# One core, two transformer blocks: the context's norm in the MLP, keys ahead of queries, borders by halves

## What is computed

```python
x = x + jnp.square(jax.nn.relu(h @ mlp_w1[i].astype(dt))) @ mlp_w2[i].astype(dt)
...
mod = (silu_c @ ada_w[i] + ada_b[i])[:, None, :]
mod_c = (silu_cc @ ada_w[i] + ada_b[i])[:, None, :]
...
h = modulate(rmsnorm_2(x, norm1_g[i]), sh1, sc1)
hc = modulate(rmsnorm_2(ctx, norm1_g[i]), csh1, csc1)
...
q, k, v = project(h)
q, k = apply_rope_2d(q, cos, sin), apply_rope_2d(k, cos, sin)
qc, kc, vc = project(hc)
k_all = jnp.concatenate([kc, k], axis=1)
v_all = jnp.concatenate([vc, v], axis=1)
...
x = x + g1 * y
x = x + g2 * swiglu(modulate(rmsnorm_2(x, norm2_g[i]), sh2, sc2), ffn_w_in[i], ffn_w_out[i])
```

## Time and profile before

| what | value |
|---|---|
| median of 3 runs | 2803.95 us (2801.78 to 2805.73) |
| the profiled execution | 2803.94 us, span of its instructions 2802.6 us |
| PE busy | 2633.5 us, 94% of the span |
| DVE, ACT, POOL busy | 1392.8, 910.1, 160.9 us |
| chain that ended last | PE 80%, DVE 11%, ACT 6% |
| mean granted TensorE clock | 0.970 of 2.4 GHz |
| DMA | 265.73 MB moved, mean 95 GB/s |
| TensorE waited for `h_lo` | 12.4 us in 11 waits (L151), 8.5 in 4 (L159) |
| TensorE waited for `w_lo` | 18.6 us in 13 waits |

### The profile page before, as it was taken

How to read it: one execution, slowest core, us unless ns; L and a number is a source line. 1 busy time by engine, 2 the same in 40 slices (tenths; PEclk the granted TensorE clock), 3 DMA queues, 4 the chain that set the end, 5 groups by cost and what they waited for, 6 DMA issues and landing times.

```text
span 2802.6 us, 34040 instructions
## 1 busy us (share of the span) xinstructions
PE 2633.5 (94%) x14886; PEld 2208.8 (79%) x14886; DVE 1392.8 (50%) x1665; ACT 910.1 (32%) x1247; POOL 160.9 (6%) x177
## 2 busy tenths in 40 slices
PE   6998999979999999999979999799999999999998
PEld 4877888878878777887868977678888788788886
DVE  5665544254465346655465257456643454443433
ACT  4332223253334432222332257432222232322222
POOL 0002210000000010000022000010000100100001
PEclk9999999999999999999989999989999999999999
DMA  3220002212333234453222100055532222223231
GB/s 117 76 90 17 28 6 76 91 61 66 115 106 121 76 119 164 154 205 125 103 84 73 63 16 1 28 181 202 207 120 90 90 91 91 90 90 105 91 101 65
DMA packets 39301, 265.73 MB, mean 95 GB/s; under 512 B 4256, under 2 KB 4640, under 8 KB 8944
## 3 DMA queue, kind: packets, MB, share of 16 engines
q1 hardware_dynamic: 29520, 205.67, 21.3%
q0 software_dynamic: 8256, 55.41, 5.7%
q10 hardware_dynamic: 1376, 2.47, 0.2%
HBM read 261.43 MB, written 2.10 MB: 94 GB/s over the span
## 4 chain that ended last, share of the span: by engine, by line
PE 80%; DVE 11%; ACT 6%; issue 2%; POOL 0%; DMA 0%; DVEq 0%; ACTq 0%
PE bank L142 79%; ACT w_hi L148 2%; DVE w_lo L151 2%; DVE ada_acc L159 1%; ACT tmp L148 1%; PE bank L145 1%; DVE tmp L159 1%; DVE dd L151 1%; ACT da_p L148 1%; DVE heads_t L159 1%; DVE da_stat L162 1%; DVE x_t L159 0%; DVE v_t L159 0%; ACT sq L148 0%; POOL sq L151 0%
## 5 line engine op out<-in xcount | busy, mean ns | idle before, releaser
L142 PE MATMUL bank<-h_hi,w_hi 128*128 128x512 f32 (+1 forms) x1992 | 805.9, 405 | 35.6 <-DVE h_lo L151 12.4
L142 PE MATMUL bank<-h_lo,w_hi 128*128 128x512 f32 (+1 forms) x1992 | 788.1, 396 | 0.0
L142 PE MATMUL bank<-h_hi,w_lo 128*128 128x512 f32 (+1 forms) x1992 | 787.7, 395 | 0.0
L151 DVE TENSOR_TENSOR w_lo<-w_raw,w_hi 128x2048 fp32r<-128x2048 f32 (+2 forms) x197 | 445.1, 2259 | 349.5 <-ACT w_hi L148 349.5
L142 PEld LDWEIGHTS bank<-h_hi,w_hi 128*128 128x128 f32 (+1 forms) x1992 | 381.5, 192 | 123.9 <-issue 20.2
L148 ACT ACTIVATE w_hi<-w_raw 128x2048 fp32r<-128x2048 f32 (+2 forms) x197 | 370.6, 1881 | 316.9 <-PE bank L142 306.8
L142 PEld LDWEIGHTS bank<-h_hi,w_lo 128*128 128x128 f32 (+1 forms) x1992 | 380.7, 191 | 83.0 <-issue 0.7
L142 PEld LDWEIGHTS bank<-h_lo,w_hi 128*128 128x128 f32 (+1 forms) x1992 | 381.6, 192 | 75.5 <-issue 0.5
L142 PE MATMUL bank<-f_hi,w_hi 128*128 128x512 f32 x672 | 262.9, 391 | 1.1 <-DVE w_lo L151 1.1
L142 PE MATMUL bank<-f_lo,w_hi 128*128 128x512 f32 x672 | 262.0, 390 | 0.0
L142 PE MATMUL bank<-f_hi,w_lo 128*128 128x512 f32 x672 | 262.0, 390 | 0.0
(11 more groups left out here) (333 smaller groups left out, 3261.1 us busy)
## 6 DMA issues: line engine op xcount, KB each, us to landing
w_raw<-in_pack_ffn SPq DMA_DIRECT2D x60, 1024.0 KB, 4.9
ada_w<-in_ada_w POOLq DMA_DIRECT2D x48, 1024.0 KB, 5.3
w_raw<-in_pack_mlp SPq DMA_DIRECT2D x32, 1024.0 KB, 5.0
w_raw<-in_pack_gdn_qkv SPq DMA_DIRECT2D x12, 1024.0 KB, 4.9
w_raw<-in_pack_sc_cu SPq DMA_DIRECT2D x8, 1024.0 KB, 5.0
w_raw<-in_pack_ffn SPq DMA_DIRECT2D x8, 768.0 KB, 4.3
w_raw<-in_pack_gdn_z SPq DMA_DIRECT2D x4, 1024.0 KB, 4.9
w_raw<-in_pack_gate_a SPq DMA_DIRECT2D x4, 1024.0 KB, 5.1
```

Of the source, the lines that this page charges most:

```text
L142: return self.engine.matmul(*a, **k) if self.engine is not None else self
L151: return self.engine.tensor_tensor(*a) if self.engine is not None else self
```

## The change

- **Context's norm.** `ctx_t` is loaded at the start of the MLP, ahead of the `ada_w` loads. The squares, the sum, the root, the spreading and the normalising run as background behind the modulation, two steps per tile; the scaling writes into `ctx_t` itself, the squares into the halves of `sq`. The gain of the context is made inside the modulation.
- **Context stage.** `da_k` stands ahead of `da_q` in the plan. TensorE makes the context's part of the first two key panels between and behind the sums and the spreading, then the part of `x`; queries come after all keys. `split_hi` and `split_lo` of the second key panel stand ahead of the norm.
- **Two waits.** `ready(k)` now gives two values: the two products with the rounded activations wait for the rounding, the third for the rest. With two tiles, four products come ahead of the second wait.
- **Halves.** Ahead of a norm, the last residual tile, its square and the last addition go by halves of 256 tokens, and the sums of a half wait for that half only.
- **Unread products.** `keep_busy` issues products whose results nobody reads: eight of 128x512 ahead of the sums of `ffn0`, `sc`, `ffn1` and the final norm, seven behind the spreading of the first three, 53 in all.

```diff
@@ -91,8 +91,8 @@
...
+        ("da_k", "da_wqkv_2", full, run_columns(D, D)),
         ("da_q", "da_wqkv_2", full, run_columns(0, D)),
-        ("da_k", "da_wqkv_2", full, run_columns(D, D)),
...
-                    T_.wait_ge(*ready(k))
+                    rounded, rest = ready(k)
+                    cut = lambda m: slice(m * P, (m + 1) * P)
+                    T_.wait_ge(*rounded)
                     for m, bank in zip(group, outs):
-                        cut = slice(m * P, (m + 1) * P)
...
+                            T_.matmul(bank[:, 0:tokens], hi[:, k, cut(m)], a_hi[:, k, 0:tokens], start=(k == 0), stop=False)
+                            T_.matmul(bank[:, 0:tokens], lo[:, k, cut(m)], a_hi[:, k, 0:tokens], start=False, stop=False)
+                    T_.wait_ge(*rest)
+                    for m, bank in zip(group, outs):
...
+                        else:
+                            done = T_.matmul(bank[:, 0:tokens], hi[:, k, cut(m)], a_lo[:, k, 0:tokens], start=False,
...
+        def last_square(self, S, ready):
+            k = self.n - 1
+            S.wait_ge(*self.added(k - 2))
+            for i, half in enumerate(TOKEN_HALVES):
+                S.wait_ge(*ready(i))
+                S.activation(self.room(k)[:, half], self.src(k)[:, half], ACT.Square, scale=self.scale_of(k)).then_inc(
+                    *up("act_square", (self.name, "half", i), *([(self.name, k)] if i else [])))
+
+        def last_add(self, V):
+            k = self.n - 1
+            V.wait_ge(*self.added(k - 1))
+            for i, half in enumerate(TOKEN_HALVES):
+                V.wait_ge(*at("act_square", (self.name, "half", i)))
+                V.tensor_tensor(self.out[:, half], self.out[:, half], self.room(k)[:, half], ALU.add).then_inc(
+                    *up("dve_sum", (self.name, "half", i), *([(self.name, k)] if i else [])))
+
...
-            T_.wait_ge(*self.added(self.n - 1))
             for c in range(self.tokens // P):
+                halves = self.on_pool and self.tokens == T
+                T_.wait_ge(*(at("dve_sum", (self.name, "half", c // 2)) if halves else self.added(self.n - 1)))
...
+            if self.in_place:
+                V.wait_ge(*at("act_square", (self.name, k)))
+            elif k >= 4:
...
-
+            return at("act_h_hi", (self.name, k)), at("dve_h_lo", (self.name, k))
...
+    ctx_sum = SquareSum("ctx", DT, CTX, sq[1][:, 0:CTX], lambda k: ctx_t[:, k, :], lambda k: loaded("ctx_loaded"),
+                        (sq[0][:, 0:CTX], sq[0][:, CTX:T]), ("act_mlp", "rstd"))
...
+                    lambda k: loaded("ctx_loaded"), in_place=True)
...
+            halves = total is not None and n == DT - 1
+            for i, part in enumerate(TOKEN_HALVES if halves else (slice(0, T),)):
+                x_part, ps = x_t[:, n, part], bank_of(tile)[:, part]
...
+                else:
+                    V.scalar_tensor_tensor(x_part, ps, col(n), x_part, ALU.mult, ALU.add).then_inc(
...
+            if halves:
+                total.last_add(V)
...
+    BUSY_SUMS, BUSY_FIRST = 8, 7
+    def keep_busy(T_, rings, name, n, key=None):
+        panel = number[key, 0, 0] if key else len(order) - 1
+        bank, before = rings.work.take(("busy", name))
+        T_.wait_ge(*freed(before))
+        T_.wait_ge(*at("act_hi", panel))
+        w = w_hi[panel % 2]
+        for _ in range(n):
+            done = T_.matmul(bank[:, :], w[:, 0:P], w[:, 0:T], start=True, stop=True)
+        done.then_inc(*up("pe_stat", ("busy", name), frees=("busy", name)))
...
+                if which and j:
+                    V.wait_ge(*at("dve_ada", ("mod", layer, j, which)))
...
-        T_.background, T_.pace = modulation_tensor(T_, rings, 0), 2
+        T_.background, T_.pace = after_another(modulation_tensor(T_, rings, 0), ctx_norm_tensor(T_, rings)), 2
...
+        G.dma_start(ctx_t[:, :, :], dram["ctx_t"].rearrange("(k p) t -> p k t", p=P)).then_inc(sems["ctx_loaded"], 16)
...
+        def keys(part, i, cs):
...
+        norms = two_norms_tensor(T_, rings)
+        keys("ctx", 0, (0,))
+        next(norms)
+        keys("ctx", 0, (1,))
+        next(norms)
+        keys("ctx", 1, (0,))
+        keys("ctx", 1, (1,))
+        keys("x", 0, (0, 1))
+        keys("x", 1, (0,))
+        keys("x", 1, (1,))
+        for i in range(2, len(where["da_k"][0])):
             for c in range(2):
...
+                keys("ctx", i, (c,))
+                keys("x", i, (c,))
+        drain(gemm_tensor(T_, rings, "da_q", h_done(da_norm)))
...
-        for _ in range(6 + DT):
+        for _ in range(DT):
...
+        split_hi(S, number["da_k", 0, 1])
         two_norms_scalar(S)
-        drain(da_norm.steps_scalar(S))
-        S.background, S.pace = ctx_norm_scalar(S), 4
+        context_keys(0, 0)
+        context_keys(0, 1)
+        for k in range(DT):
+            da_norm.round_hi(S, k)
+            if k == 3:
+                context_keys(1, 0)
+                context_keys(1, 1)
+        for i in range(len(where["da_k"][0])):
+            if i:
+                split_hi(S, number["da_k", 0, i] + 1)
+            for c in range(2):
+                if i >= 2:
+                    context_keys(i, c)
...
+        split_lo(V, number["da_k", 0, 1])
...
+        keep_busy(T_, rings, f"ffn{layer} sums", BUSY_SUMS, f"ffn1_{layer}")
         ffn_sum[layer].over_partitions(T_, rings)
         ffn_sum[layer].spread(T_, rings)
+        keep_busy(T_, rings, f"ffn{layer} first", BUSY_FIRST, f"ffn1_{layer}")
...
+        keep_busy(T_, rings, "fin sums", BUSY_SUMS)
```

More of the change, by code:

```diff
@@ L731, in evacuate @@
                 more(n)
-            if total is not None:
+            if total is not None and n == DT - 1:
+                total.last_square(S, lambda i: at("dve_x", (key, block, "half", i)))
+            elif total is not None:
                 total.square(S, n)
@@ L2352, in context_tensor @@
     def context_tensor(T_, rings):
-        two_norms_tensor(T_, rings)
-        T_.background, T_.pace = ctx_norm_tensor(T_, rings), 4
-        drain(gemm_tensor(T_, rings, "da_q", h_done(da_norm)))
-        T_.finish()
-        for i in range(len(where["da_k"][0])):
+        def keys(part, i, cs):
             n = number["da_k", 0, i]
             hi, lo = panel_view(n)
+            a_hi, a_lo, width, norm = (c_hi, c_lo, CTX, ctx_norm) if part == "ctx" else (h_hi, h_lo, T, da_norm)
             T_.wait_ge(*at("dve_lo", n))
-            for c in range(2):
-                cut = slice(c * P, (c + 1) * P)
-                for part, a_hi, a_lo, width, norm in (("ctx", c_hi, c_lo, CTX, ctx_norm), ("x", h_hi, h_lo, T, da_norm)):
-                    tile = ("da_k", part, i, c)
-                    bank, before = rings.gemm.take(tile)
-                    T_.wait_ge(*freed(before))
-                    for k in range(DT):
-                        T_.wait_ge(*norm.done(k))
-                        T_.matmul(bank[:, 0:width], hi[:, k, cut], a_hi[:, k, :], start=(k == 0), stop=False)
-                        T_.matmul(bank[:, 0:width], hi[:, k, cut], a_lo[:, k, :], start=False, stop=False)
-                        done = T_.matmul(bank[:, 0:width], lo[:, k, cut], a_hi[:, k, :], start=False, stop=(k == DT - 1))
-                    ends = [("panel", n)] if c and part == "x" else []
-                    done.then_inc(*up("pe_tile", tile, *ends))
@@ new lines, in keys @@
+            outs = []
+            for c in cs:
+                bank, before = rings.gemm.take(("da_k", part, i, c))
+                T_.wait_ge(*freed(before))
+                outs.append((c, bank[:, 0:width], slice(c * P, (c + 1) * P)))
+            for k in range(DT):
+                rounded, rest = norm.done(k)
+                T_.wait_ge(*rounded)
+                for c, out, cut in outs:
+                    T_.matmul(out, hi[:, k, cut], a_hi[:, k, :], start=(k == 0), stop=False)
+                    T_.matmul(out, lo[:, k, cut], a_hi[:, k, :], start=False, stop=False)
+                T_.wait_ge(*rest)
+                for c, out, cut in outs:
+                    done = T_.matmul(out, hi[:, k, cut], a_lo[:, k, :], start=False, stop=(k == DT - 1))
+                    if k == DT - 1:
+                        ends = [("panel", n)] if c and part == "x" else []
+                        done.then_inc(*up("pe_tile", ("da_k", part, i, c), *ends))
@@ L2399, in ctx_norm_scalar @@
     def ctx_norm_scalar(S):
-        for _ in range(6):
-            yield
         for k in range(DT):
@@ L2599, in attend_tensor @@
         next(steps)
[L2600 removed]
+        drain(beside(gemm_tensor(T_, rings, "da_o", lambda k: (at("act_da", ("hi", k)), at("dve_da", ("lo", k)))), steps, 1))
     def attend_scalar(S):
```

123 lines of the change are left out of this document (61 added, 62 removed).

## The result

The changed kernel takes 2770.88 us in the median (2768.67 to 2772.57, 4 runs) against 2803.7 (2801.78 to 2805.73); the ratio is 0.9881, 95% interval 0.9865 to 0.9897. Timed once more on the chip of the first experiments it took 2771.25 (2768.87 to 2771.8) against 2804.18: 0.9882, interval 0.9867 to 0.9896. The forecast was 2772.3 us.

A forecast was written before the change was run, and what follows sets the result against it. TensorE was taken to bound the kernel, through its waits and low clock. From 2803.94 us, -25.0 (context), +6.7 (MLP), -6.0 (`da_o`), -6.3 (borders) and -1.0 (end) sum to -31.6, giving 2772.3 us, range 2764 to 2780.

The forecast's parts named there:

- Context stage, -25.0 forecast: From the last MLP product through the queries: waits, moved work and low-clock time go, 25.3 us less 0.3 for rope.
- The six waits of 17.3 us: Context stage: TensorE's waits of 2.35, 1.23, 0.84, 2.75, 7.93 and 2.20 us go, being covered by context key tiles.
- the moved 2.5: Context stage: the 2.5 us stretch from the context's sums to the next query product moves into the MLP.
- The rope rival: Context stage: TensorE waits out a `w_lo` (2.29 us) at three panels, so the stage gives 18, total 2779.2 us; chance 0.15.
- MLP, +6.7 forecast: MLP's last block: TensorE stops between context sums and spreading, 4.7 us with spreading, plus 2.0 of slow products; bounds 0 and 8.
- the 4.2 summed: MLP stop: scaling 0.75, square and rounding 1.36, table load 1.28, small activation 0.20, root and inverse 0.64 us.
- one of the signs that I had named for being wrong: MLP: VectorE's backlog stops TensorE anywhere other than at the forecast wait ahead of the context's spreading.
- The prediction's sentence on the Trainium skill, ScalarE: Activation LUTs, section What ACT_TABLE_LOAD costs: MLP stop: the page adds about 1.38 us drain per table switch; the trace's row does not, and the forecast followed it.
- `da_o`, -6.0 forecast: `da_o`: five loops each 1.0 us shorter (3.99 to 2.95), first product 0.9 earlier, nothing behind the eighth; bounds -4 and -6.5.
- Borders, -6.3 forecast: Three borders into `ffn1_0`, `sc_cu`, `ffn1_1`: 2.1 us each, the rest becoming a wait for `w_lo`; bounds 3.6 and 14.
- The rival that unread products hold no clock: Borders and end: the clock falls despite the fillers, borders give 3.6 and the end 0.6, total 2775.4 us; chance 0.17.
- Slower, by a low clock that stays in the MLP: MLP: the clock stays low after the stop until the block ends, 14 tiles, 67 us, total 2837; chance 0.02.

The follow-up runs named there:

- The last-step run: The changed kernel, but in the last step of two tiles made together the first tile's three products stand ahead of the second's: 2767.33 us, ratio 0.9866.
- the two runs that moved such steps: Context's spreading four background steps later, against the changed kernel: 2765.67 us; modulation's sums two steps later, against a kernel of three combined edits (2747.24 us): 2732.41 us.

## Why the prediction was right, and where its terms were off

*Context stage, -25.0 forecast, -27.4 measured.* The six waits of 17.3 us and the moved 2.5 went in full. The clock's part was too small: I counted ten products behind each pause and 1.5 us for the spreading. Behind each pause stood eleven product starts, the first 0.56 apart (4.6 instead of 4.0), and the sixteen spreading products lost 2.1: eight take 0.85 to the next row at the high clock, where I had set about their duration of 1.05. The 0.3 kept for rope were not needed. The last 0.9 were in no term: 0.2 at the sums, which ran slower before, and 0.7 at the products beside the pauses, most of it since a bracket begins at the end of the product ahead of it, 0.39 us behind its start (1446.57 in the earlier trace rows), and not 0.23 behind it, the distance of starts. The rope rival fell: no row between 1434.69 and 1617.69 has a wait.

*MLP, +6.7 forecast, +8.7 measured.* The mechanism of the stop was right, and the run with the spreading a tile later showed it: 3.41 us idle of the 4.2 summed (0.5 of the difference are the sums, which run in that time), five slow products instead of ten, and 4.8 us less when it was gone. What failed was the sentence that the new order of three products costs nothing because no wait stands behind them. The waits behind them were at VectorE, not at TensorE: a pair's first tile was handed over two products later (VectorE waited 5.37 us for it, not 4.92), and with the two waits alone the MLP was 2.8 us longer. The last-step run put the waits back; of the 2.8 us its profile shows 1.5 in the MLP. So one of the signs that I had named for being wrong, VectorE stopping TensorE elsewhere in the MLP, came in part.

The prediction's sentence on the Trainium skill, ScalarE: Activation LUTs, section What ACT_TABLE_LOAD costs, can be read again: here too the next activation starts 0.02 us after the load (1354.43 + 1.28 to 1355.73), and the rounding ahead of it ends 0.01 us before it. The trace does not agree with the page's further 1.38 us.

*`da_o`, -6.0 forecast, -4.8 measured.* The steps won 4.6 us (3.07 each instead of 2.95), and the wait for `w_lo` is as forecast (2.08). Not forecast: behind that wait nine products run slow, 1.4 us net; before, at 1.18 us of waiting, they did not. The first product comes 1.6 us earlier where I had 0.9, but 1.1 of that is luck, in a place that the change does not touch. At the start of the attention, before and after:

```profile
1640.98 2.93 PE L142 MATMUL bank<-da_k,da_q 64*128 64x256 f32 x8 [3.83 <-ACT da_p L148]
```

```profile
1624.89 1.84 PE L142 MATMUL bank<-da_k,da_q 64*128 64x256 f32 x8 [3.83 <-ACT da_p L148]
```

Behind the same wait the same eight products take 2.93 us in one profile and 1.84 in the other. In the runs with the spreading a tile later, with the last step tile by tile and without unread products they are at 2.93 again, and attention with `da_o` takes 207.5 to 207.8 us instead of 206.3. So the change itself won some 3.7 us here, and the kernel before with the two waits alone 4.0. The stretches around the wait for `w_lo`, of the changed kernel:

```profile
1785.00:1789.00 4.00, 2.11 (x8) 1.42 (x8) 2.79 (x3) 2.28 (x2) 0.00 (x0) 1.00 0.00 0
1789.60:1793.50 3.90, 3.84 (x10) 3.03 (x11) 1.40 (x4) 3.06 (x3) 1.29 (x1) 0.56 0.74 252
```

*Borders, -6.3 forecast, -7.9 measured.* Halves (0.6), spreading (0.9) and the new wait for `w_lo` were as forecast. The slack of 0.6 us until `w_lo` binds was read from ScalarE's first tile row; TensorE's own second panel started at 1866.72, 1.1 us behind `w_lo`. Five tenths for each of three borders are the whole difference. The second panel before, without a bracket:

```profile
1866.72 0.39 PE L142 MATMUL bank<-h_hi,w_hi 128*128 128x512 f32 x1
```

The rival that unread products hold no clock fell at the sums and is half true behind the spreading (without the seven, two borders of three had slow products): there the clock does fall without them, and the wait for `w_lo` hid it at one border and not at the other.

*Slower, by a low clock that stays in the MLP:* fell. Four or five products were slow, in other runs eleven.

*Stages held at no change.* The -0.9 between the memory's norm and the MLP is there with the two waits alone too (214.7 us instead of 215.6). The -1.7 of the rest lies in the first FFN, where the first wait for `ada_acc` fell from 1.24 to 0.77 us and the thirteen slow products behind it are gone (the second such wait grew from 0.72 to 1.18).

Errors of +2.0 (MLP), +1.2 (`da_o`), -2.4 (context), -1.6 (borders) and -2.6 (stages held at no change, but for the first) nearly cancel with the +3.4 of the first stage's clock. That the total was met to 1.4 us is luck: the terms were off by up to 2.6 us each, and the second profile of the same kernel, whose first stage took 823.8 us, is 35.2 us shorter than the kernel before, not 31.6.

## What to carry to other kernels

Where tiles are made in pairs, look at what the pair's order hands to the next engine, and at how many steps of background work fall into one place: a sum or a spreading that stands in the same place as the last step of its input stops the array, one tile later the stop is gone (some 20 us here, over the two runs that moved such steps). Moving work into idle time was worth the wait it covered plus the clock behind it (3.65 and 2.85 us in the context stage). When a wait on a prepared operand is hidden, follow its chain to the next place that it is needed: at the borders and in `da_o` most of the gain stayed, in the MLP it came back as the next wait for VectorE's `w_lo`.

## What the runs showed of the hardware

The clock makes equal work unequal. The first stage took 823.3 to 829.5 us in the changed kernel and the kernels that differ from it only further on, and most of the difference lies around one norm. Stretches of the second profile of the changed kernel and of the run with eight unread products (columns as in the earlier trace rows):

```profile
433.00:448.00 15.00, 14.73 (x89) 13.04 (x90) 4.86 (x6) 4.74 (x8) 0.00 (x0) 1.00 0.21 71
```

```profile
433.00:448.00 15.00, 14.03 (x57) 11.80 (x56) 2.48 (x2) 4.86 (x7) 0.00 (x0) 0.66 0.21 71
```

The mean granted clock is 1.00 in one, 0.66 in the other, of its two levels 2.4 and 1.2 GHz, and 57 instructions of TensorE fit where 89 did, behind the same wait of 0.97 us and the same small products. At the start of the attention the same wait of 3.83 us was followed by eight products in 2.93 or in 1.84 us. The length of a pause does not tell alone what follows: 2.75 us ahead of `w_lo` left the clock high, 1.76 behind a spreading and 2.08 in `da_o` were followed by nine products at the low one. What a pause costs here is its length and, as a chance, some 2 us more (an estimate: ten products, each 0.20 us longer).
